# Three layer norms: the second token tile turned into accumulator banks, and a weight split moved between two additions

## What is computed

```python
def rms_norm(x, g):
    xf = x.astype(jnp.float32)
    y = xf * lax.rsqrt(jnp.mean(xf * xf, axis=-1, keepdims=True) + NORM_EPS)
    return (y * g).astype(x.dtype)

def first_block(x, ...):
    for i in range(DEPTH):                      # DEPTH = 2
        h = rms_norm(x, ln_attn_g[i])
        dq, dk, dv, mq, mk, mv = jnp.split(h @ w_in[i], cuts, axis=-1)
        ...
        x = x + jnp.concatenate([y_diff, y_moba], axis=-1) @ w_out[i]
        x = x + conv_ffn(rms_norm(x, ln_ffn_g[i]), w_up[i], conv_w[i], conv_b[i], w_down[i])
    return x
```

## Time and profile before

| what | us |
|---|---|
| median of three runs | 2056.38 |
| lowest, highest | 2055.04, 2061.04 |
| profiled execution | 2060.76 |
| its span on the core | 2058.9 |
| TensorE busy in the span | 1926.6 |
| VectorE, ScalarE, GpSimd busy | 1132.2, 863.8, 210.3 |

### The profile page before, as it was taken

One profiled execution on the slowest core, in us unless ns is written; L12 is line 12 of the kernel. 1 busy time (PEld: TensorE's weight loads), 2 busy tenths in 40 slices (PEclk: granted clock), 3 DMA queues, 4 the chain that ended last, 5 costly groups with the idle time before them and its releaser, 6 DMA issues. The chain is left out here.

```text
span 2058.9 us, 36819 instructions
## 1 busy us (share of the span) xinstructions
PE 1926.6 (94%) x15696; PEld 1615.2 (78%) x15696; DVE 1132.2 (55%) x1798; ACT 863.8 (42%) x1531; POOL 210.3 (10%) x249
## 2 busy tenths in 40 slices
PE   7998999899899999989999998999999879888998
PEld 5756998685699978856898987888877678677987
DVE  6554775465567655466556665544444545536643
ACT  5353664345456543445322334322222243545532
POOL 1100221020012200101113311000000101000000
PEclk9987999999799999999999999999999989998999
DMA  7682665458456552335000032333323214014653
GB/s 261 203 307 83 187 184 192 141 177 307 142 144 185 178 169 86 99 109 183 3 24 4 4 124 62 114 110 95 113 84 100 62 63 138 25 43 134 190 186 123
DMA packets 231641, 264.53 MB, mean 128 GB/s; under 512 B 14214, under 2 KB 153782, under 8 KB 231095
## 3 DMA queue, kind: packets, MB, share of 16 engines
q1 hardware_dynamic: 230891, 261.36, 40.1%
q10 hardware_dynamic: 588, 0.82, 0.1%
HBM read 261.07 MB, written 1.09 MB: 127 GB/s over the span
## 5 line engine op out<-in xcount | busy, mean ns | idle before, releaser
L401 PE MATMUL acc<-rounded,rounded 128*128 128x512 f32 (+1 forms) x2552 | 883.8, 346 | 24.7 <-DVE rounded L653 11.0
L402 PE MATMUL acc<-rounded,rounded 128*128 128x512 f32 (+1 forms) x2552 | 874.9, 343 | 0.0
L403 PE MATMUL acc<-rounded,rounded 128*128 128x512 f32 (+1 forms) x2552 | 874.1, 342 | 0.0
L385 DVE TENSOR_TENSOR rounded<-arena,rounded 128x2048 fp32r<-128x2048 f32 (+1 forms) x194 | 434.2, 2242 | 299.4 <-ACT rounded L374 299.3
L401 PEld LDWEIGHTS acc<-rounded,rounded 128*128 128x128 f32 x2552 | 488.0, 191 | 93.8 <-issue 20.5
L402 PEld LDWEIGHTS acc<-rounded,rounded 128*128 128x128 f32 x2552 | 488.1, 191 | 60.4 <-issue 1.9
L403 PEld LDWEIGHTS acc<-rounded,rounded 128*128 128x128 f32 x2552 | 487.5, 191 | 60.4
L374 ACT ACTIVATE rounded<-arena 128x2048 fp32r<-128x2048 f32 (+1 forms) x194 | 363.0, 1874 | 349.4 <-PE acc L403 308.4
L1406 DVE SCALAR_TENSOR_TENSOR arena<-acc,pcol,arena 128x254 f32<-128x254 f32 (+1 forms) x176 | 76.8, 478 | 52.3 <-ACT arena L1387 50.8
L823 PEld LDWEIGHTS sc<-arena 128*128 128x128 f32 x592 | 72.8, 196 | 37.9 <-ACT arena L929 20.4
L1990 PE MATMUL sc<-arena 64*64 64x64 f32 x2560 | 95.6, 224 | 6.9 <-DVE arena L2140 5.8
(11 more groups left out here) (243 smaller groups left out, 1691.8 us busy)
## 6 DMA issues: line engine op xcount, KB each, us to landing
arena<-in_w_ff SPq DMA_DIRECT2D x64, 1024.0 KB, 5.3
arena<-in_w_ada SPq DMA_DIRECT2D x48, 1024.0 KB, 5.2
arena<-in_w_up SPq DMA_DIRECT2D x88, 512.0 KB, 5.1
arena<-in_w_in SPq DMA_DIRECT2D x24, 1024.0 KB, 5.2
arena<-in_w_down SPq DMA_DIRECT2D x20, 1024.0 KB, 5.1
arena<-in_w_out SPq DMA_DIRECT2D x16, 1024.0 KB, 5.1
arena<-in_w_in_even SPq DMA_DIRECT2D x9, 1024.0 KB, 5.4
arena<-in_w_in_odd SPq DMA_DIRECT2D x8, 1024.0 KB, 5.3
```

Of the source, the lines that this page charges most:

```text
L385: dve.tensor_tensor(r32(w), w, r32(high_slot(c)[:, 0:size(c)]), ALU.subtract).then_inc(split_made, 1)
L401: pe.matmul(ps, ah, bh, start=first, stop=False)
L402: pe.matmul(ps, ah, bl, start=False, stop=False)
L403: return pe.matmul(ps, al, bh, start=False, stop=last)
```

## The change

It has two parts. First, for the norms of qkv in layer 1 and of the up projection in both layers, tile 1's transposes go to two banks of the pool "acc" instead of "tr", and `norm_dve` scales both tiles before any low part. Since fills are numbered through the program, each such norm takes two numbers of the acc pool (and two fewer of tr), and the accumulators behind it use the banks shifted by two. Second, `add_dve` no longer makes all splits of the second half before the additions: the last one stands between the addition of tile 0 and that of tile 1. This holds for all four calls (w_out and w_down of both layers).

```diff
+        TWO_POOLS = {("attn", 1): "acc", ("ffn", 0): "acc", ("ffn", 1): "acc"}
+
         def plan_norm(key):
             norm_n[key] = len(norm_n)
-            stage(("norm", key), tr=4)
+            stage(("norm", key), **({"tr": 2, TWO_POOLS[key]: 2} if key in TWO_POOLS else {"tr": 4}))
...
         def norm_fill(key, tt, half):
 
-            return tr_at[("norm", key)] + 2 * tt + half
+            if key in TWO_POOLS and tt:
+                return TWO_POOLS[key], {"acc": acc_at, "sc": sc_at}[TWO_POOLS[key]][("norm", key)] + half
+            return "tr", tr_at[("norm", key)] + 2 * tt + half
+
+        def norm_turned(eng, key, tt):
+
+            pool, f = norm_fill(key, tt, 1)
+            eng.wait_ge(POOLS[pool][1], f + 1)
...
             for half in range(2):
-                ps = claim(pe, "tr", norm_fill(key, tt, half))
+                pool, f = norm_fill(key, tt, half)
+                ps = claim(pe, pool, f)
                 for k in range(4):
                     kt = 4 * half + k
                     ins = pe.transpose(ps[:, k * P:(k + 1) * P], xn[:, tt, kt * P:(kt + 1) * P], ident)
-                ins.then_inc(tr_full, 1)
+                ins.then_inc(POOLS[pool][1], 1)
...
             for n, norm in enumerate(norms):
                 if n >= scaled:
                     norm_scale(dve, norm, 0)
-                if not norm[4]:
+                early = not norm[4] and norm[0] not in TWO_POOLS
+                if early:
                     norm_low(dve, norm, 0, 0)
                 if n >= scaled:
                     norm_scale(dve, norm, 1)
                 for tt in range(TT):
                     for half in range(2):
-                        if norm[4] or tt or half:
+                        if not early or tt or half:
                             norm_low(dve, norm, tt, half)
...
         def add_dve(dve, key, kts, after=None):
 
-            def add(hf):
+            g, n = chunk_at[key], -(-kts // 4)
+            for hf in range(2):
+                for i in range(n - 1 - hf):
+                    ahead_dve(dve, g + n * hf + i + HIGH)
                 for tt in range(TT):
                     f = acc_at[key] + 2 * hf + tt
                     ps = filled(dve, "acc", f)
                     x = h_lat[:, tt, hf * 512:(hf + 1) * 512]
                     dve.tensor_tensor(x, x, ps[:, :], ALU.add).then_inc(drain("acc", f), 1)
+                    if hf and tt == 0:
+                        ahead_dve(dve, g + 2 * n - 2 + HIGH)
                 if after:
                     after(hf)
-
-            tok_walk(dve, ahead_dve, key, kts, 2, add, last=False)
+                if not hf:
+                    ahead_dve(dve, g + n - 1 + HIGH)
```

More of the change, by code:

```diff
@@ L599, in norm_scale @@
                 before = [k for k in norm_n if norm_n[k] == norm_n[key] - 1][0]
-                dve.wait_ge(tr_full, norm_fill(before, tt, 1) + 1)
+                norm_turned(dve, before, tt)
             dve.wait_ge(norm_rstd, n + 1)
@@ L625, in norm_high @@
                 f, hi, lo, cols = norm_quarter(norm, tt, 1)
-                ps = filled(act, "tr", f)
+                ps = filled(act, *f)
                 for k, (kt, c) in enumerate(cols):
                     ins = act.activation(lo[:, k, :], ps[:, c], ACT.Identity, bias=shift(kt), scale=gain(kt))
-                ins.then_inc(drain("tr", f), 1)
+                ins.then_inc(drain(*f), 1)
             for half in range(2):
@@ L632, in norm_high @@
                 if shift:
-                    wait_drained(act, "tr", f)
+                    wait_drained(act, *f)
                     ins = act.activation(r32(hi), lo, ACT.Copy)
                 else:
-                    ps = filled(act, "tr", f)
+                    ps = filled(act, *f)
                     for k, (kt, c) in enumerate(cols):
@@ L645, in norm_low @@
             if shift and half == 0:
-                ps = filled(dve, "tr", f)
+                ps = filled(dve, *f)
                 for k, (kt, c) in enumerate(cols):
                     ins = dve.tensor_scalar(lo[:, k, :], ps[:, c], gain(kt), shift(kt), ALU.mult, ALU.add)
-                ins.then_inc(drain("tr", f), 1)
+                ins.then_inc(drain(*f), 1)
             dve.wait_ge(norm_high_set, 2 * norm_tile(key, tt) + half + 1)
             if shift:
-                wait_drained(dve, "tr", f)
+                wait_drained(dve, *f)
                 dve.tensor_tensor(r32(lo), lo, r32(hi), ALU.subtract).then_inc(mod_norm_done, 1)
@@ L655, in norm_low @@
                 for k, (kt, c) in enumerate(cols):
-                    ins = dve.scalar_tensor_tensor(r32(lo[:, k, :]), bank("tr", f)[:, c], gain(kt), r32(hi[:, k, :]), ALU.mult, ALU.subtract)
-                ins.then_inc(drain("tr", f), 1)
+                    ins = dve.scalar_tensor_tensor(r32(lo[:, k, :]), bank(*f)[:, c], gain(kt), r32(hi[:, k, :]), ALU.mult, ALU.subtract)
+                ins.then_inc(drain(*f), 1)
         def norm_dve(dve, *norms, scaled=0):
@@ L678, in norm_ready @@
             else:
-                wait_drained(pe, "tr", norm_fill(key, tt, half))
+                wait_drained(pe, *norm_fill(key, tt, half))
         def tok_gemm(pe, key, f, kts, blocks, lhsT, ready=None, before=None, pieces=None):
```

## The result

The change took 2048.62 us (median of 22 runs, 2041.58 to 2066.75), the kernel before 2059.05 beside it (22 runs, 2055.01 to 2064.53): 10.4 us less, a ratio of 0.9950 with a 95% interval of 0.9938 to 0.9963. Forecast were 8.7 us less. The profiled execution of the change took 2050.45, its span 2048.6; the span before was 2058.9.

What follows compares the result with a forecast made beforehand. TensorE, busy 94% of the span, was taken as the bound, so only its standstills count. Gains of 2.1 + 2.1 + 2.1 + 2.4 = 8.7 us from the median 2056.38 gave 2047.7 us, range 2043 to 2053.

Steps and rivals of the forecast that it cites:

- P4: Layer norm into the second block: early first addition brings tile 0's scale and transposes forward, 2.4 us gained.
- P1: Layer norm into the first up projection: tile 1's earlier scale restarts TensorE sooner, 2.1 us gained (2.03 to 2.41).
- P3: Layer norm into the second up projection: same program order and pattern as P1, 2.1 us gained.
- P2: Layer norm into the second layer's qkv: first addition ahead of the split, 2.1 us gained after a charge.
- The charge for tile 0's low part: At P2, tile 0's first low half waits behind tile 1's scale; gain 2.1 to 2.2, without it 2.3 to 2.7.
- The rise of the clock stays where it is: Rival behind P1 to P3: restart earlier but clock rises at the old time; gain 5.7 us, 2050.7; chance 0.16.
- The clock does not fall: Rival at P1 to P3: clock keeps its level through the shorter waits, 6.9 us more gained, 2040.8; chance 0.06.
- The weights eat P2 and P4: Rival: TensorE reaches chunks not yet split, so only P1 and P3 count; gain 4.2 us, 2052.2; chance 0.14.
- The clock falls elsewhere: Slower rival: shifted pauses bring new clock falls, 4.8 us each, in second-layer attention or second block; 2067; chance 0.04.

Runs made afterwards that it cites:

- with fillers: The change plus transposes of the unit matrix in TensorE's waits at P1, P2 and P3; 2047.41 us (6 runs), ratio 0.994 to the kernel before.
- e_late: The change with the moved split later: behind tile 0's low parts at P2, behind both scales at P4; 2052.52 us (12 runs), ratio 0.997 to before.

## Why the prediction was right, and where its terms were off

Measured were 10.4 us against 8.7 forecast, with 2048.6 inside 2043 to 2053. The mechanism was right at all four places, but for what GpSimd does at them (P4 below). Counted from the end of the last matmul, as the text does, the restarts were 7.51 at P1 (7.4 to 7.8 forecast), 7.10 at P3 (earlier than the same range) and 6.35 at P2 (6.8); at P4 0.39 us of idle time stayed where none was forecast. TensorE's idle time fell by 7.5 against about 9, because the text took the whole of a gap for idle time: 2.1 of the 9.7 are transposes that ran shorter. The sum of 8.7 is 9.7 in the trace, and each term was off by a little. The ends of the single terms add up to 8.6 to 9.4, not to the 8.3 to 9.5 written; 9.7 is outside both.

**P1, 2.1 forecast, 2.33 measured.** The step is "square at 187.48, power over at 189.85 (2.37 behind)". The square came where the text had it (1.24 behind the last matmul, against 1.29), but its scale followed 2.26 behind it (185.21 to 187.47), not 2.51. In the earlier trace rows L589 of tile 1, whose row I had not read out, took 0.47 because the scale of tile 0 stood beside it; in the change that scale is over by then and L598 takes 0.22. So the step copied a delay that the change itself removes. The clock was at the slow end of what the text allowed: it fell at 187.8, before the second turn (188.28) and not just behind it.

**P3, 2.1 forecast, 2.72 measured.** I took P3 to repeat P1. Its program does, its clock does not: there the second turn took 1.09 (1.97 at P1) and the restart fell within full clock. The window shows that the lower level came later and was short:

```profile
556.00:559.80 3.80, 1.70 (x14) 1.50 (x14) 3.80 (x16) 3.80 (x12) 0.00 (x0) 1.00 0.22 53
560.00:563.20 3.20, 3.20 (x16) 3.20 (x16) 2.29 (x1) 0.50 (x1) 0.00 (x0) 0.50 0.00 0
563.50:573.00 9.50, 9.50 (x83) 9.50 (x82) 4.04 (x5) 3.64 (x5) 0.00 (x0) 1.00 0.41 113
```

**P2, 2.1 forecast, 2.58 measured.** The charge for tile 0's low part, queued behind tile 1's scale, was put at 0.2 to 0.6. It is 0.08: the first half was ready some 1.18 behind L648's start (385.32 to 386.50), and VectorE reached it at 386.58. The scale was early for the same reason as at P1, and tile 1's addition came 0.1 earlier against the last matmul than in the earlier trace rows. The clock helped: eight transposes took 1.09, not 1.97. This outweighed what GpSimd lost.

**P4, 2.4 forecast, 2.08 measured, and the one step that was wrong in kind.** I wrote that tile 0's scale would be bound by VectorE, 0.64 behind the start of tile 1's addition, because the power would be ready before that (by 0.5 in the text's own sum at P2). It comes 0.95 behind it (751.98 to 752.93), released by L600: GpSimd's mean was over only 0.08 behind the split. I had costed the split's new neighbour at nothing and named VectorE's queue alone. The Trainium skill has the rule (SBUF — State Buffer, Who interferes with whom): a VectorE instruction with two SBUF inputs and a GpSimd instruction that reads SBUF exclude each other, and the later one waits for the whole of the earlier. The trace agrees for a GpSimd instruction that comes second (0.93 beside the split, 0.22 alone). Beside a scale it is 0.44 to 0.77 in these traces; the same section has that kind of operation among those that can shut GpSimd out. That puts the step's error at 0.3 us: the hold costs this much where tile 0's scale is waited for, at P2 and P4, since VectorE itself is busy with tile 1's addition for the rest of it, and nothing at P1 and P3, where it hides behind tile 1. (e_late's 0.8 at P2 are this and the split out of VectorE's way; no run has the one without the other.)

**The rivals.** "The rise of the clock stays where it is" was partly true at P1. Behind the restart the clock stayed at 0.50 for 6.1 us (191.87 to 198.0) in place of 4.9, and 0.5 of the 2.33 went back on the way to P2. At P2 the rise moved with the restart (4.9 us behind it, 5.0 before), and at P3 it came sooner (4.2 behind it, 5.0 before), so there the rival did not hold. "The clock does not fall" held nowhere in the change; with fillers it did hold at P1 to P3, and there it brought 6.9 us over the change (3.2, 2.2 and 1.5, of which 0.4 are gaps), about what the rival said (6.9 beside the gaps); in that profile the attentions took most of it again. "The weights eat P2 and P4" fell: the shift behind each of them stands in the table. "The clock falls elsewhere" happened in the last attention: there the change is at 0.50 from 1737 to 1751 and from 1785 to 1789, and loses 3.5. The 3.2 that the attention behind P4 gave nearly paid for it.

**The total.** That 10.4 lies so near 9.7 owes something to chance: in the profiles 2.2 us came from the first attention, and in the second block 1.9 more went than came. That the median itself, 2048.6, is within 1 us of the 2047.7 forecast is luck as well: the three runs from which the text started had a median of 2056.38, 2.7 below that of all 22, and the gain was 1.7 larger than the forecast.

## What to carry to other kernels

- A bank and an order are one edit: free the bank alone and the engine waits for the data, move the data alone and it waits for the bank (0.0 and 0.5 us alone, 1.6 together at P1).
- When an instruction moves, ask which small instruction of another engine will stand beside it in time, not only what is queued behind it; here a 0.2 us mean on GpSimd became 0.9 beside a 2.3 us split on VectorE. Copy no delay from the trace of before without asking whether its cause stays.
- Where single times scatter by more than the effect, measure the gap at each edited place from one trace of each kernel: the gaps of the same kernel repeated to 0.01 us while its profiled spans differed by 4. Between different kernels allow for the clock in the gap, up to 0.4 us here.

## What the runs showed of the hardware

- GpSimd's 128x1 instruction L598 took 0.22 us alone, 0.93 or 0.94 beside a VectorE split and 0.44 to 0.77 beside a scale. At all four places of the change it ended 0.08 to 0.09 us behind the split's end.
- TensorE's granted clock stayed at 1.00 (2.4 GHz) through the waits of P1 to P3 when they held transposes of the unit matrix at 0.12 us each. It did so although gaps of up to 0.8 us were left between them. I had given the same clock a chance of 6 in 100 in the plain change, where it fell each time.
- The granted clock in unchanged stretches differed between kernels and between runs of one kernel (0.69 to 0.86 in the first attention; the last matmul in front of P1 started between 182.27 and 188.09 in the profiles, with nothing changed ahead of it). These differences were larger than most effects studied here.
